# Cache turns of one unit per branch in NSA attention, keys loaded a second time in paired layout, the next maximum ahead of the weighting on VectorE, block products on GpSimd

## The reference

```python
for i in range(DEPTH):
    g = norm_g[i]
    kind, j = i % N_MIXERS, i // N_MIXERS
    xp = half_ffn(xp, g[0], g[1], ffn_w_in[i, 0], ffn_w_out[i, 0])
    xs = half_ffn(xs, g[0], g[1], ffn_w_in[i, 0], ffn_w_out[i, 0])
    hp, hs = rms_norm(xp, g[2]), rms_norm(xs, g[2])
    ...   # kind 0: short_conv, 1: nsa_prompt and nsa_sample, 2: diff_prompt and diff_sample
    xp = xp + rms_norm(yp, g[3])
    xs = xs + rms_norm(ys, g[3])
    xp = half_ffn(xp, g[4], g[5], ffn_w_in[i, 1], ffn_w_out[i, 1])
    xs = half_ffn(xs, g[4], g[5], ffn_w_in[i, 1], ffn_w_out[i, 1])
```

## Time and profile before

| what | value |
|---|---|
| median of the runs shown | 2251.08 us (2248.93 to 2254.98, 3 runs) |
| the profiled execution, its own time | 2253.68 us |
| its span, first to last instruction | 2252.0 us |
| mean granted TensorE clock | 0.98 of full |
| busy, share of the span | PE 95%, DVE 63%, ACT 42%, POOL 8% |
| nsa's attention loop | about 806 to 917 us of the span |
| diff's attention loop | about 1432 to 1483 us |

### The profile page before, as it was taken

One profiled execution on the slowest core, in us unless ns is written; L12 is line 12 of the kernel. 1 busy time (PEld: TensorE's weight loads), 2 busy tenths in 40 slices (PEclk: granted clock), 3 DMA queues, 4 the chain that ended last, 5 costly groups with the idle time before them and its releaser, 6 DMA issues.

```text
span 2252.0 us, 42235 instructions
## 1 busy us (share of the span) xinstructions
PE 2147.7 (95%) x17682; PEld 2078.9 (92%) x17682; DVE 1422.3 (63%) x1600; ACT 937.3 (42%) x1113; POOL 180.6 (8%) x203
## 2 busy tenths in 40 slices
PE   7999999999999977799999999779999999999998
PEld 6999999999999954699999999669999999999998
DVE  5774877656664566366647655557665765687663
ACT  4443454344433334254444444325443444435442
POOL 3000110001000132010001001101000000101000
PEclk9999999999999979699999999989999999999999
DMA  6555445554554445035545555523554555454551
GB/s 214 187 175 181 152 150 187 186 184 135 186 187 169 159 161 206 23 128 187 192 164 160 177 178 173 192 94 118 186 202 149 171 175 181 165 170 147 186 199 49
DMA packets 286443, 370.79 MB, mean 165 GB/s; under 512 B 12304, under 2 KB 212417, under 8 KB 286245
## 3 DMA queue, kind: packets, MB, share of 16 engines
q1 hardware_dynamic: 282682, 365.11, 48.5%
q10 hardware_dynamic: 3626, 3.74, 0.5%
HBM read 364.87 MB, written 8.11 MB: 166 GB/s over the span
## 4 chain that ended last, share of the span: by engine, by line
PE 68%; DVE 15%; issue 11%; ACT 4%; DMA 1%; POOL 1%; SPq 0%; ACTq 0%; DVEq 0%; POOLq 0%
PE ps L1444 21%; PE ps L1446 21%; PE ps L1445 20%; DVE w_low_ring L908 4%; DVE y L1418 2%; DVE x L1424 2%; ACT w_high_ring L667 1%; DVE y L1018 1%; ACT probs L753 1%; DVE small L1173 1%; DMA wstage<-in_cache_nsa_dram 1%; PE ps L1466 1%; PE ps L1452 1%; DVE probs L1187 1%; DVE x_lo L965 1%
## 5 line engine op out<-in xcount | busy, mean ns | idle before, releaser
L1444 PE MATMUL ps<-x_hi,w_high_ring 128*128 128x264 f32 x3112 | 889.2, 286 | 9.4 <-DVE w_low_ring L908 9.4
L908 DVE TENSOR_TENSOR w_low_ring<-wstage,w_high_ring 128x2048 fp32r<-128x2048 f32 x332 | 728.5, 2229 | 265.0 <-ACT w_high_ring L667 185.5
L1446 PE MATMUL ps<-x_hi,w_low_ring 128*128 128x264 f32 x3112 | 884.6, 284 | 0.0
L1445 PE MATMUL ps<-x_lo,w_high_ring 128*128 128x264 f32 x3112 | 883.6, 284 | 0.0
L1444 PEld LDWEIGHTS ps<-x_hi,w_high_ring 128*128 128x128 f32 x3112 | 586.3, 188 | 12.1 <-DVE w_low_ring L908 8.4
L1445 PEld LDWEIGHTS ps<-x_lo,w_high_ring 128*128 128x128 f32 x3112 | 587.8, 189 | 0.0
L1446 PEld LDWEIGHTS ps<-x_hi,w_low_ring 128*128 128x128 f32 x3112 | 586.7, 189 | 0.0
L1444 PE MATMUL ps<-h_hi,w_high_ring 128*128 128x264 f32 x1664 | 474.9, 285 | 6.7 <-issue 4.6
L1446 PE MATMUL ps<-h_hi,w_low_ring 128*128 128x264 f32 x1664 | 474.7, 285 | 0.0
L1445 PE MATMUL ps<-h_lo,w_high_ring 128*128 128x264 f32 x1664 | 473.3, 284 | 0.0
L667 ACT ACTIVATE w_high_ring<-wstage 128x2048 fp32r<-128x2048 f32 (+2 forms) x172 | 306.5, 1816 | 295.0 <-PE ps L1446 284.0
(11 more groups left out here) (296 smaller groups left out, 1778.5 us busy)
## 6 DMA issues: line engine op xcount, KB each, us to landing
wstage<-in_ffn_w_in_dram SPq DMA_DIRECT2D x352, 512.0 KB, 5.0
wstage<-in_ffn_w_out_dram SPq DMA_DIRECT2D x160, 512.0 KB, 4.6
wstage<-in_conv_w_in_dram SPq DMA_DIRECT2D x48, 512.0 KB, 4.7
wstage<-in_nsa_w_in_dram SPq DMA_DIRECT2D x20, 512.0 KB, 4.6
wstage<-in_ffn_w_out_dram SPq DMA_DIRECT2D x32, 256.0 KB, 3.4
wstage<-in_conv_w_out_dram SPq DMA_DIRECT2D x16, 512.0 KB, 4.7
wstage<-in_cache_nsa_dram SPq DMA_DIRECT2D x16, 512.0 KB, 4.9
wstage<-in_diff_w_in_dram SPq DMA_DIRECT2D x16, 512.0 KB, 5.3
```

What stands on the lines that cost most here:

```text
L908: V.tensor_tensor(w_low_ring[:, u % RING, 0:n, 0:cols], wstage[:, stage_of["w", u] % RING, 0:n, 0:cols], w_high_ring[:, u % RING, 0:n, 0:c ...
L1444: MM(out, wh, hi, start=first, stop=False)
L1445: MM(out, wh, lo, start=False, stop=False)
L1446: return MM(out, wl, hi, start=False, stop=last)
```

## The change

A turn of nsa now takes one unit of each branch: the selected branch of sample n and the window of sample n + 4 (modulo 8). SP loads the keys of both a second time, straight from the cache, in 64-column pieces, into the free half of the window's slot (`paired_keys`), with a semaphore pair of their own; PE turns them from there, and GpSimd's `k_pairs` copies go away. GpSimd takes the block product of every turn (three buffers instead of two), DVE's `compress` goes away, and `sum_blocks` and `add_blocks` run in iterations 3, 5, 7 and 9. On DVE an iteration begins with `task_max(n)` and `copy_keys(n)`, and ends with `task_mix(n-1)`; this holds for diff too. On ACT the values' copy moves ahead of the second half of the keys. Renamed semaphores and placements are left out of the diff below.

```diff
@@ -459,7 +457,7 @@
                 return [(n, 0, n)]
-            return [(2 * n + x, n % 2, n // 2 + 4 * x) for x in range(2)]
+            return [(2 * n, 0, n), (2 * n + 1, 1, (n + 4) % DEC)]
@@ -467,6 +465,12 @@
             return wstage[:, t % RING, 0:2, :].rearrange("p t (g c) -> p t g c", g=GROUPS)
+        def paired_keys(n):
+            t = stage_of["c", 2 * n + 1]
+            return wstage[:, t % RING, 2:4, :].rearrange("p a (b g d) -> p a b g d", b=2, g=GROUPS)
@@ -611,29 +615,20 @@
                     for n in range(TURNS):
-                        for kt in range(2 if s.kind == "nsa" else 0):
-                            if n:
-                                pool.wait_ge(cache_turned, 2 * n - 1 + kt)
-                            for x, (u, br, b) in enumerate(turn_units("nsa", n)):
-                                t = stage_of["c", s.cache0 + u]
-                                pool.wait_ge(loaded[t % RING], 32 * (t // RING + 1))
-                                k0 = 0 if br else P
-                                nc.gpsimd.tensor_copy(k_pairs[:, kt, x, :, :],
-                                                      cache_pages("nsa", t, br)[:, kt, :, k0:k0 + HEAD]).then_inc(keys_paired, 1)
-                        if s.kind == "nsa" and n % 2 == 0:
-                            u, _, b = turn_units("nsa", n)[0]
-                            t = stage_of["c", s.cache0 + u]
+                        if s.kind == "nsa":
+                            t = stage_of["c", s.cache0 + 2 * n]
                             pool.wait_ge(loaded[t % RING], 32 * (t // RING + 1))
-                            if n:
-                                pool.wait_ge(cache_summed, n // 2)
+                            if n >= 3:
+                                pool.wait_ge(cache_summed, (n - 3) // 2 + 1)
                             page = wstage[:, t % RING, :, :].rearrange("p (t g) (h c) -> p (t g h) c", t=2, c=256)
-                            nc.gpsimd.tensor_tensor(prod_dec[:, 0, :, :, :].rearrange("p t g c -> p (t g) c"), page[:, :, 0:P],
-                                                    cmp_w_tok[:, :].unsqueeze(1).broadcast_to([P, 8, P]), ALU.mult)\
-                                .then_inc(prod_even, 1)
+                            nc.gpsimd.tensor_tensor(prod_dec[:, n % 3, :, :, :].rearrange("p t g c -> p (t g) c"), page[:, :, 0:P],
+                                                    cmp_w_tok[:, :].unsqueeze(1).broadcast_to([P, 8, P]), ALU.mult)                                .then_inc(cache_prod, 1)
                         t, dst, src = cache_values(s.kind, n, 1 if s.kind == "nsa" else 0)
                         pool.wait_ge(loaded[t % RING], 32 * (t // RING + 1))
-                        nc.gpsimd.tensor_copy(dst, src).then_inc(kept_odd, 1)
+                        nc.gpsimd.tensor_copy(dst, src).then_inc(kept_last, 1)
                     pool.wait_ge(cache_scored, 2 * (turn0[s.kind] + TURNS))
+                    if s.kind == "nsa":
+                        pool.wait_ge(cache_summed, TURNS // 2)
                     nc.gpsimd.memset(pt_wide[1][:, :, :], 0.0).then_inc(wide_zeroed, 1)
@@ -727,7 +722,7 @@
                     act.wait_ge(loaded[t % RING], 32 * (t // RING + 1))
-                    nc.scalar.activation(dst, src, ACT.Copy).then_inc(kept_even, 1)
+                    nc.scalar.activation(dst, src, ACT.Copy).then_inc(kept_first, 1)
@@ -754,6 +749,8 @@
                                                  accum_out=esum[:, m % 4, i:i + 1]).then_inc(at_exp, 1)
+                    if kind == "nsa" and n < TURNS:
+                        keep_values(n)
                     if n < TURNS:
@@ -773,8 +770,6 @@
                             .then_inc(cmp_exp, 1)
-                    if kind == "nsa" and n < TURNS:
-                        keep_values(n)
                 rounds = ROUNDS[kind]
@@ -1227,18 +1222,6 @@
-                def compress(n):
-                    u, _, b = turn_units("nsa", n)[1]
-                    t = stage_of["c", s.cache0 + u]
-                    dve.wait_ge(loaded[t % RING], 32 * (t // RING + 1))
-                    if n:
-                        dve.wait_ge(cache_summed, n // 2)
-                    page = wstage[:, t % RING, :, :].rearrange("p (t g) (h c) -> p (t g h) c", t=2, c=256)
-                    V.tensor_tensor(prod_dec[:, 1, :, :, :].rearrange("p t g c -> p (t g) c"), page[:, :, 0:P],
-                                    cmp_w_tok[:, :].unsqueeze(1).broadcast_to([P, 8, P]), ALU.mult)\
-                        .then_inc(prod_odd, 1)
                 def add_blocks(k):
@@ -1250,10 +1233,6 @@
                 for n in range(len(tasks) + 3):
-                    if 1 <= n <= len(tasks):
-                        task_mix(n - 1)
-                    if n >= 3:
-                        task_add(n - 3)
                     if n < len(tasks):
@@ -1262,15 +1241,16 @@
                         keep_rows()
-                    if kind == "nsa":
-                        if n == 0:
-                            shift_compressed()
-                        if n == 1:
-                            weigh_compressed()
-                        if n < TURNS and n % 2:
-                            add_blocks(n // 2)
-                        if n < TURNS and n % 2 == 0:
-                            compress(n)
+                    if n >= 3:
+                        task_add(n - 3)
+                    if kind == "nsa" and n in (3, 5, 7, 9):
+                        add_blocks(n // 2 - 1)
+                    if 1 <= n <= len(tasks):
+                        task_mix(n - 1)
+                    if kind == "nsa" and n == 0:
+                        shift_compressed()
+                    if kind == "nsa" and n == 1:
+                        weigh_compressed()
@@ -1585,7 +1565,6 @@
                     pe.wait_ge(cmp_probs, 1)
-                    pe.wait_ge(blocks_added, 1)
                     for qt in range(2):
@@ -1667,18 +1646,18 @@
                         pe.wait_ge(keys_second, m)
-                    for x, (u, br, b) in enumerate(turn_units(kind, n)):
-                        t = stage_of["c", s.cache0 + u]
-                        if kind == "nsa":
-                            pe.wait_ge(keys_paired, 4 * n + 2 * kt + x + 1)
-                        elif kt == 0:
-                            pe.wait_ge(loaded[t % RING], 32 * (t // RING + 1))
-                        for e in range(2 if kind == "nsa" else 4):
-                            if kind == "nsa":
-                                i, keys = 2 * e + x, k_pairs[:, kt, x, 2 * e:2 * e + 2, :].rearrange("p g d -> p (g d)")
-                            else:
-                                i, keys = e, cache_pages(kind, t, br)[:, kt, e, 0:P]
-                            mm = TR(ps[:, 7, P * i:P * i + P], keys, ident[:, :])
+                    if kind == "nsa":
+                        pe.wait_ge(keys_loaded[n % 2], 64 * (n // 2 + 1))
+                        for x, (u, br, b) in enumerate(turn_units(kind, n)):
+                            for e in range(2):
+                                col = P * (2 * e + b // 4)
+                                mm = TR(ps[:, 7, col:col + P], paired_keys(n)[:, x, kt, 2 * e:2 * e + 2, :]
+                                        .rearrange("p g d -> p (g d)"), ident[:, :])
+                    else:
+                        t = stage_of["c", s.cache0 + n]
+                        pe.wait_ge(loaded[t % RING], 32 * (t // RING + 1))
+                        for g in range(GROUPS):
+                            mm = TR(ps[:, 7, P * g:P * g + P], cache_pages(kind, t, 0)[:, kt, g, 0:P], ident[:, :])
                     mm.then_inc(cache_turned, 1)
@@ -1686,23 +1665,26 @@
                     pe.wait_ge((keys_first, keys_second)[kt], m + 1)
-                    _, br, b = turn_units(kind, n)[0]
-                    col = SEQ * br + P * kt
                     for quad in range(4):
-                        mm = MM(ps[32 * quad:32 * quad + 32, 5, col:col + P], q_wide[kind][:, quad, 32 * b:32 * b + 32],
+                        if kind == "nsa":
+                            _, br, b = [unit for unit in turn_units(kind, n) if unit[2] // 4 == quad % 2][0]
+                            col, window = SEQ * br + P * kt, 32 * (b % 4)
+                        else:
+                            col, window = P * kt, 32 * n
+                        mm = MM(ps[32 * quad:32 * quad + 32, 5, col:col + P], q_wide[kind][:, quad, window:window + 32],
                                 kt_dec[kind][:, kt, quad, :], start=(n == 0 and kt == 0), stop=True, skip_group_check=True)
...
-                    pe.wait_ge(prod_even, k + 1)
-                    pe.wait_ge(prod_odd, k + 1)
+                    pe.wait_ge(cache_prod, 2 * k + 2)
                     for x in range(2):
-                        b = k + 4 * x
+                        b = 2 * k + x
                         for i in range(4):
...
```

(38 more changed lines are left out.)

12 lines of the change are left out of this document (5 added, 7 removed).

## The result

The changed kernel takes 2337.03 us (median of 4 runs, 2334.35 to 2339.49), the kernel before 2250.01 us beside it (4 runs, 2246.94 to 2254.98): a ratio of 1.0381, 95% interval 1.0359 to 1.0404. It is 87 us slower where 44 were forecast, and 11 us above the end of the range. The sign and the loop that was named are right; the sizes are not.

What follows compares the result with a forecast made beforehand. PE was taken to bound nearly the whole span, but DVE and ACT taking turns the attention loops. Terms 10 (long nsa) + 4 (turns) + 14 (diff) + 16 (clock) = +44 us on 2251: 2295 us, range 2266 to 2326.

Steps and rivals of the forecast that it cites:

- The loop: In nsa's and diff's task loops, DVE - ACT - DVE becomes DVE - PE - DVE: PE's whole leg enters the path.
- The order's sum: DVE's new order: +10 us in nsa's long tasks, +4 in nsa's turns, +14 in diff; 28 us together.
- the step with the last sum of blocks: In nsa's long tasks, the step with the last sum_blocks, at n = 9, on the path: 7.6 us.
- The clock's term: PE's pauses in nsa's and diff's loops lower its granted clock: +16 us, a third of the bound.
- The bound of 50: Upper bound of the clock loss: 1.6 times on all 24 PE legs of 3.5 us on average, 50 us.
- One product and one copy, hidden: GpSimd's work per nsa turn, about 4 us beside a turn of 7 us, costs nothing.
- Loads hidden but for the first: In nsa's turns, loads of 6 us hide under 7.5; only the first makes PE wait, about 3 us.
- the upper end: Loads in nsa's turns: a start that isn't covered in the odd turns, 2 us each, costs 6 more.
- Max-first overlaps: Rival: in nsa and diff, DVE works under ACT's 2.00 us; 31 us faster, 2220 us; chance 8%.
- The turns did not balance the order: Rival: gains from products and keys in nsa's turns balance the order's cost; within 7 us of 2251; chance 5%.
- The small pieces' 2341 us: Rival: small key loads bind nsa's turns at 17.8 us, 62 us on top of 28, about 2341 us; chance 5%.
- Clock low on all legs: Rival: all PE legs in nsa's and diff's loops run at the lower clock level, 2329 us; chance 10%.

Runs made afterwards that it cites:

- after: The changed kernel with the whole change, measured against the kernel before: 2337.03 us, ratio 1.0381.

## Why the prediction was wrong, by its own steps

The 85.8 us of the two traces, by cause:

| cause | worked out from | us | forecast |
|---|---|---|---|
| order on DVE at the full clock | long 57.1 - 43.8; diff 51.5 - 39.7 + 5.3; turns 3.0 + 19.4 - 4.4 - 5.8 - 4.8 | 13.3 + 17.1 + 7.4 = 37.8 | 28 |
| lower clock | 15.4 + 13.7 + 4.4 (extra matmuls) | 33.5 | 16 |
| loads that PE waits for in the turns | its idle time in after: 3.6 + 1.4 + 0.8 | at most 5.8 | 0 |
| products beside DVE | 71.3 - 66.5 | 4.8 | 0 |
| behind the loops | | 3.9 | 0 |

The order's part in the turns is what the other rows leave, and net of what the new turns save, such as the 10.6 us in which PE stood for key copies in the kernel before.

- **The loop, right.** DVE - PE - DVE, shown by the waits of after and by the old order, which takes the whole loss away. The step of a long nsa task, costed at 7.4 us, took 7.3 to 7.4 with the clock held up; diff's, costed at 8.6, took 8.2 to 8.7. An even turn, 6.8, took 7.0. In after itself, at the lower clock, the long steps took 8.9 to 10.2 and diff's up to 10.9, over the 7 to 9.5 and 8 to 10 that were to show it.
- **The order's sum, 10 us short.** What was costed too low lies at the edges: with the clock held up, the step with the last sum of blocks took 9.3 to 9.5 us and not 7.6, and diff's short steps 6.1 to 7.4, 6.9 on average and not 6.4.
- **The clock's term, the main miss: 16 us taken, 33.5 measured.** The bound of 50 was sound. The choice of a third of it was not: it was made because a fall seen before covered only part of a leg. But there a fall came once, after one pause; here each pause is followed by the next, and the clock was low on some part of nearly every leg. The range allowed for three quarters of the bound, 37 us, and so held the clock; it did not hold it together with the other misses.
- **"One product and one copy, hidden": wrong.** The cover was counted as time on GpSimd, where there is enough. It isn't there that the product costs: it delays DVE's instructions, and the order of the semaphores starts it just when DVE's are on the path. The earlier trace rows held the sign already, with DVE's own product at 2.70 us beside GpSimd's; in the first turn, where GpSimd had none, it took 1.22 (812.67). The Trainium skill (SBUF — State Buffer, SBUF: two separate sides) says that a DVE instruction with two inputs in SBUF, the on-chip memory of `wstage`, and a GpSimd instruction that reads SBUF lock each other out for a whole instruction; the trace agrees, as the small multiplication ends with the product, 0.02 us apart.
- **Loads hidden but for the first: the first was left out of the sum, and two odd turns weren't covered.** The prediction calls the first load's wait of about 3 us counted in the turns' 4 us, but its steps of 6.8 and 8.3 us hold no wait; it took 3.6. In two of the three odd turns PE waited 1.4 and 0.8 us, where the upper end allowed 2 each. A turn's loads were taken at 6 us. In the turn shown the keys came 9.8 us after the first issue (844.18 to 853.96): SP issues eight loads one after the other, and a window load of 256 KB lands 4.9 us after its issue (4.4 in the kernel before; medians of 12). No run took these waits away.
- **The rivals.** Max-first overlaps was wrong for this kernel for the reason given, PE's program order; with the scores issued ahead it comes true in the long tasks, at 4.6 us a step. The turns did not balance the order, which costs 79 us by itself. The small pieces' 2341 us come nearest in number, but by chance: with the new turns alone the kernel takes 2252. Clock low on all legs, 2329 us, is nearest in its mechanism and was short by the products, the loads and the edges; its 50 us of clock were 33.5.

Two things stay open. The 3.9 us behind the loops weren't tried; in the 25 us behind diff's loop the granted clock was 0.59 in after and 0.80 in the kernel before. And the parts of the turns can't be told apart to better than some 2 us: the run with all extra matmuls gained 11 us in its median, 5 in the executions that were profiled (2305.45 and 2300.27) and 4.4 in the turns of its trace.

## What to carry to other kernels

When an instruction is moved ahead of another on an in-order engine, follow what it waits for through the other engines' program orders: if that comes from behind the instruction it overtook, a loop is closed, and each engine on it runs alone. Where such a loop makes TensorE pause in every step, cost its leg at the lower clock on most steps, and not as one would after a single pause. Reorder both ends together, the consumer's order and the producer's, and only in the stage where no other work (here the cache turns) hangs on the same queue.

## What the runs showed of the hardware

- Extra matmuls that compute nothing made the kernel faster: 2337 to 2299 us with up to 8 a task, since PE stood there anyway and, in the long tasks, its next leg ran at 1.00 instead of 0.57 to 0.77 of the clock.
- A DVE instruction on 4 elements per partition took 1.93 us beside a GpSimd product that reads the same memory, and 0.17 us beside none. Beside a store of zeros by GpSimd, which reads nothing, it stayed at 0.17 (a store at 897.89, 2.02 us, the multiplication at 898.35 in after). That isn't so for every instruction: in the kernel before, the negation of the maximum (L1176, 4 elements, one input) took 1.19 us beside such a store (869.13 to 870.32, the store 868.28 to 870.30) and 0.17 beside nothing, and in after the reciprocal of 4 elements took 0.17 beside the very product (857.18).

```profile
868.28 2.02 POOL L637 MEMSET pt_wide_b<- 128x2304 f32 x1 [4.20 <-PE ps L1692]
869.13 1.19 DVE L1176 TENSOR_SCALAR small<-small 128x4 f32<-128x4 f32 x1
```
